# Two-layer retention and attention model on one Trainium2 core: the row scaling of the second even-mixer softmax done by GpSimd

## The reference, cut to what matters

```
for qs in range(0, seq, Q_BLOCK):            # two blocks of 128 query rows
    s = einsum('bqhd,bkhd->bhqk', q[:, qs:qe], k[:, :qe]) * scale
    s = s + cum_logf[:, :, qs:qe, None] - cum_logf[:, :, None, :qe]
    p = softmax(where(causal, s, -inf), axis=-1)
    outs.append(einsum('bhqk,bkhd->bqhd', p, v[:, :qe]))
```

## Time and profile before

| | |
|---|---|
| median of 3 timed runs | 1912.83 us |
| lowest and highest of them | 1910.91 and 1914.89 us |
| span of the profiled execution, first to last instruction | 1908.4 us |
| what lies around it, by the median of the runs | 4.4 us |
| PE busy | 1880.6 us, 99% of the span |
| DVE busy | 1300.4 us, 68% |
| ACT busy | 1119.2 us, 59% |
| POOL busy | 330.9 us, 17% |
| mean granted TensorE clock | 0.999 of full speed |

### The profile page before, as it was taken

How to read it: one execution, slowest core, us unless ns; L and a number is a source line. 1 busy time by engine, 2 the same in 40 slices (tenths; PEclk the granted TensorE clock), 3 DMA queues, 4 the chain that set the end, 5 groups by cost and what they waited for, 6 DMA issues and landing times.

```text
span 1908.4 us, 24906 instructions
## 1 busy us (share of the span) xinstructions
PE 1880.6 (99%) x9073; PEld 1622.1 (85%) x9073; DVE 1300.4 (68%) x1919; ACT 1119.2 (59%) x1685; POOL 330.9 (17%) x559
## 2 busy tenths in 40 slices
PE   9999999999999999999999899999999999999999
PEld 7888888888888888888887688888888887788888
DVE  6687776666776776666568775776666578856664
ACT  6486555555866654655466665654555466665552
POOL 1110123111101441022100000431122111101220
PEclk9999999999999999999999999999999999999999
DMA  8866689868657997688865454997788787646884
GB/s 281 245 198 189 202 256 293 266 222 251 194 183 217 288 287 230 189 254 254 237 185 183 133 188 139 285 278 232 229 257 253 213 268 239 202 149 193 253 256 140
DMA packets 283497, 429.97 MB, mean 225 GB/s; under 512 B 25028, under 2 KB 161440, under 8 KB 283120
## 3 DMA queue, kind: packets, MB, share of 16 engines
q1 hardware_dynamic: 256144, 352.41, 59.8%
q0 software_dynamic: 26768, 75.64, 14.6%
q10 hardware_dynamic: 464, 0.34, 0.1%
HBM read 393.15 MB, written 35.15 MB: 224 GB/s over the span
## 4 chain that ended last, share of the span: by engine, by line
PE 86%; DVE 6%; ACT 4%; DMA 2%; issue 1%; POOL 0%; ACTq 0%; DVEq 0%
PE M L955 27%; PE M L957 27%; PE M L956 27%; DVE WL L1479 2%; ACT WH L1217 1%; PE AUX L999 1%; PE AUX L1186 1%; DMA TG<-squares 1%; PE AUX L1164 1%; DMA squares<-TG 1%; DVE SM L1665 1%; ACT TMP L1252 0%; DVE TMP L1622 0%; DMA RAW<-in_w_in 0%; PE AUX L1013 0%
## 5 line engine op out<-in xcount | busy, mean ns | idle before, releaser
L1479 DVE TENSOR_TENSOR WL<-RAW,WH 128x1024 fp32r<-128x1024 f32 (+1 forms) x670 | 810.5, 1215 | 447.9 <-ACT WH L1217 445.8
L1217 ACT ACTIVATE WH<-RAW 128x1024 fp32r<-128x1024 f32 (+1 forms) x670 | 704.1, 1054 | 528.7 <-PE M L957 480.5
L955 PE MATMUL M<-WH,Bh 128*128 128x512 f32 x1792 | 689.2, 385 | 2.0 <-DVE Bl L1506 1.7
L956 PE MATMUL M<-WL,Bh 128*128 128x512 f32 x1792 | 679.9, 379 | 0.0
L957 PE MATMUL M<-WH,Bl 128*128 128x512 f32 x1792 | 679.9, 379 | 0.0
L955 PEld LDWEIGHTS M<-WH,Bh 128*128 128x128 f32 x1792 | 339.2, 189 | 52.2 <-issue 3.2
L957 PEld LDWEIGHTS M<-WH,Bl 128*128 128x128 f32 x1792 | 339.1, 189 | 48.1
L956 PEld LDWEIGHTS M<-WL,Bh 128*128 128x128 f32 x1792 | 339.2, 189 | 45.8
L1247 ACT ACTIVATE AS<-M,KEEP 128x256 f32<-128x256 f32 x132 | 55.3, 470 | 78.3 <-PE M L957 78.2
L955 PE MATMUL M<-WH,MTh 128*128 128x512 f32 x128 | 52.9, 413 | 0.0
L1894 POOL TENSOR_TENSOR KEEP<-SM,KEEP 128x2 f32<-128x2 f32 x15 | 10.6, 710 | 219.9 <-DVE SM L1533 219.9
(11 more groups left out here) (473 smaller groups left out, 2741.4 us busy)
## 6 DMA issues: line engine op xcount, KB each, us to landing
RAW<-in_ffn_w_in SPq DMA_DIRECT2D x352, 256.0 KB, 3.8
RAW<-in_w_in SPq DMA_DIRECT2D x103, 512.0 KB, 4.7
RAW<-in_w_gate_up SPq DMA_DIRECT2D x176, 256.0 KB, 4.4
RAW<-in_ffn_w_out SPq DMA_DIRECT2D x88, 512.0 KB, 4.6
RAW<-in_w_down SPq DMA_DIRECT2D x44, 512.0 KB, 4.7
RAW<-in_x_w_kv SPq DMA_DIRECT2D x32, 512.0 KB, 4.6
RAW<-in_even_w_in SPq DMA_DIRECT2D x24, 512.0 KB, 4.5
RAW<-in_odd_w_in SPq DMA_DIRECT2D x24, 512.0 KB, 5.2
```

The lines of the kernel that those rows point to most:

```text
L955: e.matmul(out, s.hi, wh, start=s.at0, stop=False)
L956: e.matmul(out, s.hi, wl, start=False, stop=False)
L1217: e.activation(p.WH[:, h, 0:s.size], p.RAW[:, i, 0:s.size], ACT.Copy).then_inc(k.w_hi, 1)
L1479: e.tensor_tensor(p.WL[:, h, 0:s.size], p.RAW[:, s.u % NRAW, 0:s.size], hi.bitcast(F32), ALU.subtract).then_inc(k.w_lo, 1)
```

## The change

The function `heads` gets a parameter for the name of the scaling step, "hg_p" as before; the even mixer passes "hg_g". A step "hg_g" has two parts. DVE waits for the sums, takes the two reciprocals and adds to a new semaphore hg_rc. GpSimd waits for it, does the two multiplications, 128x128 and 128x256, with the same operands as DVE did, and adds to a second new semaphore, shares. The transpose on PE waits for shares. The planned times, banks and buffers stay as they were, and the odd mixer keeps "hg_p".

```
--- before.py
+++ after.py
@@ -645,7 +645,7 @@
                     x.final = s
         self.residual(f"w_out{l}", B, KD, f"mg{l}_", 0.5, lambda kt: self.gain(16 + 8 * l + kt), f"f{l}_")
 
-    def heads(self, at, gap, lab_o, names, V, Q, K, vals, extra, A, tail):
+    def heads(self, at, gap, lab_o, names, V, Q, K, vals, extra, A, tail, scaled="hg_p"):
 
         for hp in range(4):
             b = at + 2 * gap * hp
@@ -661,10 +661,10 @@
                 s.e = self.tmp(s)
                 ss.append(s)
             for hh, s in enumerate(ss):
-                f = self.add("hg_p", b + 4.2 + 1.2 * hh)
+                f = self.add(scaled, b + 4.2 + 1.2 * hh)
                 f.s = s
                 t = self.add("pt", b + 5.6 + 1.2 * hh + late)
-                t.source, t.maker, t.e = "hg_p", f, s.e
+                t.source, t.maker, t.e = scaled, f, s.e
                 s.e.final = t
                 t.x = self.tmp(t)
                 pts.append(t)
@@ -744,7 +744,7 @@
         c = self.chunk("av", B, 0, KD, lab)
         av = self.values(c, nm, [VA[:, t, :] for t in range(T)])
         self.CT, self.ct = S["CT"], ct
-        self.heads(c.end + 1.3, 2.65, lab_o, ["aq0", "aq1", "ak0", "ak1"], VA, QA, KA, av, S["NB"], A, 0.0)
+        self.heads(c.end + 1.3, 2.65, lab_o, ["aq0", "aq1", "ak0", "ak1"], VA, QA, KA, av, S["NB"], A, 0.0, "hg_g")
 
     def odd_mixer(self, S, lab, lab_o):
         A, QD, KD_, VD, CB, U = (S[x] for x in ("A", "QD", "KD", "VD", "CB", "U"))
@@ -890,6 +890,7 @@
         self.hq_sq, self.hq_sum, self.hx_made = sem("hq_sq"), sem("hq_sum"), sem("hx")
         self.cu_y, self.cu_ln, self.cu_lf = sem("cu_y"), sem("cu_ln"), sem("cu_lf")
         self.row_max, self.probs, self.bo_made = sem("row_max"), sem("probs"), sem("bo")
+        self.hg_rc, self.shares = sem("hg_rc"), sem("shares")
         self.cv_y, self.cv_hi, self.cv_lo = sem("cv_y"), sem("cv_hi"), sem("cv_lo")
         self.zeroed, self.x_fin = sem("zeroed"), sem("x_fin")
         self.su_gain, self.su_sum, self.su_exp, self.su_ang, self.su_abs, self.su_cos, self.su_sin, self.su_lam, self.su_tab = (
@@ -1117,7 +1118,10 @@
                 e.matmul(x[:, 128:384], z.q[:, P:256], z.k[:, 0:256], start=True, stop=True).then_inc(k.aux_full[z.bank], 1)
                 e.matmul(aux[:, 128:384], s.q[:, P:256], s.k[:, 0:256], start=True, stop=True).then_inc(k.aux_full[b], 1)
         elif s.kind == "pt":
-            e.wait_ge(k.probs, s.maker.p_n)
+            if s.source == "hg_g":
+                e.wait_ge(k.shares, s.maker.n)
+            else:
+                e.wait_ge(k.probs, s.maker.p_n)
             if s.use > 1:
                 e.wait_ge(k.aux_out[b], s.use - 1)
             x = p.TMP[s.e.i]
@@ -1765,6 +1769,10 @@
             e.scalar_tensor_tensor(out=x0[:, 0:128], in0=x1[:, 0:128], scalar=s.nl[:, 0:1], in1=x0[:, 0:128], op0=ALU.mult, op1=ALU.add)
             e.scalar_tensor_tensor(out=x0[:, 128:384], in0=x1[:, 128:384], scalar=s.nl[:, 1:2], in1=x0[:, 128:384], op0=ALU.mult,
                                    op1=ALU.add).then_inc(k.probs, 1)
+        elif s.kind == "hg_g":
+            q = s.s
+            e.wait_ge(k.aux_out[q.bank], q.use)
+            e.reciprocal(q.rc, q.sm).then_inc(k.hg_rc, 1)
         elif s.kind in ("hg_p", "cx_p"):
             q = s.s
             x = p.TMP[q.e.i]
@@ -1913,6 +1921,12 @@
                 q = 8 if x.by_t else 4
                 e.dma_start(x.rows[32 * c:32 * c + 32, :].rearrange("p (q e) -> p q e", q=q),
                             p.parked[x.slot, c * n:(c + 1) * n].rearrange("(q j e) -> j q e", q=q, j=32)).then_inc(k.d_hx[x.slot], 16)
+        elif s.kind == "hg_g":
+            q = s.s
+            x = p.TMP[q.e.i]
+            e.wait_ge(k.hg_rc, s.n)
+            e.tensor_scalar(x[:, 0:128], x[:, 0:128], q.rc[:, 0:1], None, ALU.mult)
+            e.tensor_scalar(x[:, 128:384], x[:, 128:384], q.rc[:, 1:2], None, ALU.mult).then_inc(k.shares, 1)
         elif s.kind == "zero":
             e.wait_ge(k.w_used, s.done)
             e.memset(s.what, 0.0).then_inc(k.zeroed, 1)
```

## The result

| | before | changed |
|---|---|---|
| median of 4 runs each | 1911.87 us | 1920.05 us |
| lowest to highest | 1910.51 to 1914.89 | 1918.67 to 1921.81 |
| profiled execution, its own time | not given | 1921.81 |
| its span | 1908.4 | 1920.0 |

The ratio is 1.0049, with a 95% interval from 1.0034 to 1.0063. The change costs 8.2 us, against 1.5 forecast, and the time lies above the stated range. The profiled execution of the changed kernel is the slowest of its four: by its span it is 11.6 us behind the profile of before. So the 4.4 us in the table of before are not what lies around a span: the profiled execution there was one of the quicker ones, some 1910.2 us (1908.4 + 1.8).

A forecast was written before the change was run, and what follows sets the result against it. PE was taken to bound the kernel. Delays of 0.75, 0 and 0.74 us at pairs 1, 2 and 3 made 1.5 us, added to the median 1912.83 for 1914.3 us; range 1911.5 to 1918.5.

The forecast's parts named there:

- the 4.4 us in the table of before: Whole kernel before: the median of the runs, 1912.83 us, stood 4.4 us above the trace's own span, 1908.4.
- What bounds the kernel, and where the chain is on the path: PE bounds, busy 1880.6 of 1908.4 us; reciprocal, multiplications and transpose delay it at two of eight transposes (1.64, 1.71 us).
- The hops: Between engines around GpSimd's multiplications: 0.08 us from DVE's reciprocal to GpSimd, 0.05 us back to PE.
- 1.25 us a head: GpSimd's two multiplications for each head: 0.55 us for 128x128 and 0.70 us for 128x256.
- the bounds: GpSimd's price for a head's two multiplications: 0.21 us at the lower end, 1.87 us at the upper.
- the three places: Late transposes: +0.75 us at pair 1's first head, 0 at pair 2's first, +0.74 at pair 3's second.
- rival 3: Pairs 1 to 3: GpSimd shut out by weight splits, at 1.87 us a head; +5.9 to 7.2 us, chance 0.08.
- The shared port: SBUF port pair of DVE and GpSimd: one trace row showed no holding, sum 1.5 us; the skill's lock rule gave Rival 2.
- Rival 2: Pairs 1 and 2: DVE's weight splits behind the reciprocals shut GpSimd out; sum +3.7 to 4.9 us, chance 0.30.
- 3c to 3c + 1.2 us: Rival 2's sum over the late transposes, for a GpSimd price of c us a head.
- The clock: PE's clock after over 4 us idle at pair 1, in rival 3: effect not shown, no price; 1.00 over the stretch before.
- No gain from DVE's relief: DVE sheds 16 multiplications, about 0.5 us a head, some 4 us in all; gain for PE costed at nothing.

The follow-up runs named there:

- e5: Changed kernel, with PE making 20, 8 and 14 extra matmuls on zeros ahead of its three longest-waiting transposes: 1917.43 us, ratio 1.0030 to before.
- e1: Changed kernel, but in pairs 1 and 2 DVE waits behind its reciprocal until GpSimd has multiplied that head: 1917.80 us, ratio 1.0030 to before.
- e4: Changed kernel, with GpSimd filling the two blocks with zeros instead of multiplying them (leaves out the scaling): 1911.18 us, ratio 1.0000 to before.
- e3: Kernel before, nothing on GpSimd, with 4 more DVE multiplications by 1.0 ahead of the first head's scaling: 1914.06 us, ratio 1.0008 to before.
- e2: The change in pairs 3 and 4 only, DVE scaling pairs 1 and 2 as before: 1913.76 us, ratio 1.0012 to before.
- m_b07: Kernel before, two planned times moved so DVE scales pair 1's first head and pair 3's second head earlier: 1908.75 us, ratio 0.9980 to before.
- m_g07: Changed kernel with the same two moves of planned times as m_b07: 1914.88 us, ratio 1.0012 to before.
- m_p3: Kernel before with only the second heads' scaling moved forward, the first move of m_b07: 1910.96 us, ratio 0.9996 to before.

## Why the prediction was wrong

- *What bounds the kernel, and where the chain is on the path*: right. The two transposes that waited before are those where the plain price shows. The odd mixer's +3.34 us stand in the one profile; the medians of the kernels above follow the stretch.
- *The hops*: right. The reciprocal row starts at 1096.77 and takes 0.16 us, GpSimd's row starts at 1097.02, 0.09 later; PE starts 0.06 us behind the end of the second (1098.52 to 1098.58).
- *"My estimate is 0.55 for 128x128 and 0.70 for 128x256, 1.25 us a head"*: 0.59 and 0.91, 1.5 us. It lay inside the bounds. Put into the sum as it stood, with 1.51 in place of 1.25, the three places give 1.01, 0.27 and 1.00 us: 2.3 in all, where I had 1.5. The measured +1.01 at the sixth head is this term alone. A slip that changes nothing: rival 3's terms add to 7.1 at their upper end, not 7.2.
- *The shared port*: this is the step that failed first. "By the row the sum stays at 1.5" took a row in which GpSimd was first and read two columns as evidence on the case where GpSimd comes second and reads 384. Rival 2 had the mechanism right, with its place, its order of start (split at 1064.29, GpSimd at 1064.42) and its size: it said +1.88 for the first transpose, measured 2.00, and +1.1 to +2.3 for pair 2, measured +1.74 to the third and, where the clock stayed at 1.00 (e5), +1.9. Its formula, 3c to 3c + 1.2 us for a price of c a head, gives 4.5 to 5.7 with the measured 1.51, and e5's stretch lost 5.57. e1 shows it by taking the split away, e4 by taking the read away. Of the waits' 5.6 us (e5) it makes about 3.3, what is left over the 2.3 of the plain price; the rows say nearly the same, with 0.96 us held at the first head, 0.91 and 0.74 at the third, and the 0.5 us that PE lost at the eighth, 3.1 in all. The Trainium skill's page "SBUF — State Buffer", section "SBUF: two separate sides", has the rule: the later one "fully blocks". The rows agree when GpSimd comes second, 0.74 to 0.96 us lost, each time until about 0.12 us before the split's row ends. They don't bear it out the other way, and there the measurement decides: with GpSimd first, DVE was held 0.11 us at 1080.38, and not visibly at 1098.15 and 1105.20 or in the earlier trace rows. So that row was read rightly for its own case; the mistake was to let it stand for the other one.
- *The clock*: the second step that failed, a term missing from the sum. Rival 3 named the idle time and gave it no price, with the remark that the clock was 1.00 over the stretch. It costs 3.7 us net in the profiles (e5), 2.4 by the medians. It can fall behind idle time of PE, whoever causes it (DVE in e3, ACT in the odd mixer), here 3.63 and 1.75 us.
- *The range*: its top, 1918.5, lies just under rival 3's 1918.7 to 1920.0, so it left that rival out. The measured 1920.05 is close to rival 3's top by luck: its dear multiplication, 1.87 us a head, was not found (1.5), and the clock, which it didn't price, made up the difference. It takes all three terms to get to the stretch's 9.24: 2.3 for the plain price, 3.3 for the port and 3.7 for the clock.
- *No gain from DVE's relief*: right. DVE's busy time in the program fell by 3.6 us, and nothing on PE started earlier for it. What did start earlier were the splits that then held GpSimd.

Open: why the clock fell in some executions and not in others. At the first and sixth transposes it fell behind 2.68 and 2.84 us (e1) and not behind 2.72 (e2, changed). Behind the odd mixer's 2.5 us it fell in the profiles of the changed kernel, e1 and e4 and not in those of before, e2, e3 and e5. Behind 3.5 us at the same place it fell in m_b07 and m_g07, and in m_p3 it stayed at 1.00.

## What to carry to other kernels

Before work is moved to GpSimd, look at what DVE runs next to it: here a GpSimd multiplication that reads SBUF (the on-chip memory that both engines work in) was held for 0.7 to 1.0 us whenever a DVE split with two SBUF operands had begun before it, and freeing DVE made just such a split start earlier. Where PE already waits, each microsecond more on the chain is paid in full, as at the sixth head here (+1.01 us for 1.0 us more), and the price of PE's idle time is to be counted with the slower clock that can follow it. And if a short step is late because of what stands ahead of it in an engine's order, move it in the order: two planned times brought 0.2% here, where the faster-looking relief of the engine cost 0.5%.

## What the runs showed of the hardware that was not expected

- A GpSimd tensor_scalar in fp32 takes 0.59 us for 128x128 and 0.91 for 128x256, thus some 0.27 us and 2.5 ns for each element of a row; DVE takes 0.29 and 0.35. A fill takes 0.20 and 0.31.
- GpSimd is let in before the split's row ends: in the first head 1.09 us into a split of 1.21, and in the other three long rows of the changed kernel, taken off their bare price, 0.12 to 0.14 us ahead of the end as well.
- A split that starts 0.39 or 0.55 us into a GpSimd multiplication of 0.60 or 0.92 us is not lengthened (1.23 and 1.22 us); one that starts 0.05 us into it takes 1.39 (e1, 1068.09). So coming second costs DVE less than it costs GpSimd.
- The clock fell behind an idle time of only 1.75 us at the third transpose, where 3.63 us of idle time and a slow stretch lay 15 us ahead, and not behind single idle times of 1.75 us in m_g07, 2.72 in e2 or 3.54 in m_p3's odd mixer.
